# Second-key one-hots of the second token tile built on GpSimd instead of VectorE and ScalarE

## What is computed

```python
s_top, i_top = lax.top_k(sc, TOPK)                    # sc: scores of 8 heads x 2 x 128 keys
cand_idx = i_top[..., 0, :, None] * N_KEYS + i_top[..., 1, None, :]
best_s, best_pos = lax.top_k(cand.reshape(T, PEER_HEADS, TOPK * TOPK), TOPK)
g = jax.nn.softmax(best_s, axis=-1)                   # idx, g: 8 heads x 16 = 128 slots a token
u = peer_u[eb]                                        # gathered rows, (token, slot, 2048)
a = jax.nn.gelu(jnp.einsum('td,tkd->tk', xb, u), approximate=False)
return jnp.einsum('tk,tkd->td', wb * a, peer_v[eb])   # sum over the 128 slots of coef * row
h = layer_norm(ALPHA * h + ffn, ln2_g[l], ln2_b[l])
```

## Time and profile before

| | us |
|---|---|
| median of three runs | 2490.89 (2490.71 to 2491.93) |
| the profiled execution, its own time | 2489.8 |
| its span in the profile | 2487.9 |
| chunks of tile 1: first one-hot to the first panel matmul | 1940.41 to 1990.56 |
| panels and gathered rows: first panel matmul to the last row added | 1990.56 to 2468.6 |
| last layer norm and output | 2468.6 to 2487.9 |

### The profile page before, as it was taken

How to read it: one execution, slowest core, us unless ns; L and a number is a source line. 1 busy time by engine, 2 the same in 40 slices (tenths; PEclk the granted TensorE clock), 3 DMA queues, 4 the chain that set the end, 5 groups by cost and what they waited for, 6 DMA issues and landing times.

```text
span 2487.9 us, 28481 instructions
## 1 busy us (share of the span) xinstructions
PE 1769.2 (71%) x9808; PEld 1451.7 (58%) x9808; DVE 1678.8 (67%) x2299; ACT 792.8 (32%) x1339; POOL 1011.9 (41%) x559
## 2 busy tenths in 40 slices
PE   7999999999999999999700000012112699999996
PEld 5888999998889888888700000011112566666663
DVE  5444455554445555557899999999999866666666
ACT  4444444344444444455300010256347600000000
POOL 0000000000000000001388888888878078888884
PEclk9999999999999999999955555555555999999998
DMA  5444465556555555546999999999999299999997
GB/s 163 131 141 145 137 189 184 185 172 196 189 187 185 186 186 187 185 150 239 354 342 352 353 356 349 348 362 344 355 360 423 75 385 411 411 409 411 411 412 292
DMA packets 217046, 674.87 MB, mean 271 GB/s; under 512 B 18784, under 2 KB 68320, under 8 KB 183520
## 3 DMA queue, kind: packets, MB, share of 16 engines
q0 software_dynamic: 57488, 393.25, 41.4%
q1 hardware_dynamic: 159456, 280.32, 33.8%
HBM read 671.42 MB, written 2.10 MB: 271 GB/s over the span
## 4 chain that ended last, share of the span: by engine, by line
PE 45%; DVE 27%; issue 15%; POOL 8%; DMA 3%; ACT 1%; DVEq 0%; POOLq 0%; ACTq 0%; SPq 0%
PE ps L413 44%; DVE junk L1545 18%; POOL v_rows L1751 7%; DMA v_rows<-in_v_gathered,idx_all 2%; POOL u_rows L1738 1%; DVE ohs L1568 1%; DMA u_rows<-in_peer_u,idx_all 1%; ACT hi L835 1%; DVE lo L1209 0%; DVE oh_k L1524 0%; DVE ohv L1528 0%; DVE ohs L1565 0%; PE ps L498 0%; DVE ij_all L1532 0%; DVE h L1583 0%
## 5 line engine op out<-in xcount | busy, mean ns | idle before, releaser
L1209 DVE TENSOR_TENSOR lo<-raw,hi 128x1024 fp32r<-128x1024 f32 x368 | 448.7, 1225 | 490.1 <-ACT hi L835 488.7
L1738 POOL DMA_INDIRECT u_rows<-in_peer_u,idx_all x256 | 597.9, 2336 | 198.6 <-issue 107.6
L1545 DVE SCALAR_TENSOR_TENSOR junk<-u_rows,h 128x2048 bf16<-128x2048 f32 x256 | 584.7, 2291 | 47.2 <-DVE best L1514 3.5
L835 ACT ACTIVATE hi<-raw 128x1024 fp32r<-128x1024 f32 x376 | 397.6, 1060 | 567.9 <-PE ps L413 565.5
L413 PE MATMUL ps<-v_raw,wt 128*128 128x368 f32 x1536 | 475.4, 472 | 2.8 <-DMA v_raw<-in_peer_v 2.0
L1751 POOL DMA_INDIRECT v_rows<-in_v_gathered,idx_all x256 | 391.1, 1528 | 151.4 <-issue 78.2
L413 PE MATMUL ps<-xh,hi 128*128 128x256 f32 (+2 forms) x1536 | 440.6, 287 | 2.6 <-ACT qkv L835 1.3
L413 PE MATMUL ps<-xh,lo 128*128 128x256 f32 (+2 forms) x1536 | 435.6, 284 | 0.0
L413 PE MATMUL ps<-xl,hi 128*128 128x256 f32 (+2 forms) x1536 | 435.0, 283 | 0.0
L1583 DVE SCALAR_TENSOR_TENSOR h<-v_rows,coef_all,h 128x944 f32<-128x944 f32 x256 | 307.6, 1201 | 172.9 <-DMA v_rows<-in_v_gathered,idx_all 171.9
L413 PEld LDWEIGHTS ps<-v_raw,wt 128*128 128x128 f32 x1536 | 291.7, 190 | 186.1 <-DMA v_raw<-in_peer_v 2.8
(11 more groups left out here) (217 smaller groups left out, 2271.7 us busy)
## 6 DMA issues: line engine op xcount, KB each, us to landing
raw<-in_w_in SPq DMA_DIRECT2D x96, 1024.0 KB, 5.4
v_raw<-in_peer_v SPq DMA_DIRECT2D x128, 552.0 KB, 7.8
raw<-in_w_in SPq DMA_DIRECT2D x64, 256.0 KB, 3.2
raw<-in_w_in SPq DMA_DIRECT2D x32, 512.0 KB, 4.6
raw<-in_p_a SPq DMA_DIRECT2D x16, 1024.0 KB, 5.0
raw<-in_p_b SPq DMA_DIRECT2D x16, 1024.0 KB, 5.1
raw<-in_w_o SPq DMA_DIRECT2D x16, 1024.0 KB, 5.1
raw<-in_peer_wq SPq DMA_DIRECT2D x16, 1024.0 KB, 6.7
```

Source lines behind the costliest of these rows:

```text
L835: return nc.scalar.activation(o, i, f, **kw)
L1209: V.tensor_tensor(raw_lo[:, hh // 2, k4, :] if kept else lo[:, hh % SLOT_N, :, :], raw[:, hh // 2, k4, :], (kept_hi(hh) if kept else hi[:, ...
L1545: V.scalar_tensor_tensor(junk[:, n % 2, :], u_rows[k % (RING if u else HEAD_RING)][:, :], 1.0, h1[:, u // PH, :], ALU.mult, ALU.mult, accu ...
L1738: Q.indirect_dma_start(u_rows[slot][:, :], None, peer_u, bass.IndirectOffsetOnAxis(ap=idx_all[:, n:n + 1], axis=0)).then_inc(u_in[slot], 16)
```

## The change

The second-key one-hots of tile 1 go to POOL for all 32 chunks, as four `tensor_scalar` with `is_equal`, one for each token, with the key as a [128, 1] operand. DVE loses its 24 `tensor_tensor`, ACT its eight `key_one_hots` (four squares and a Relu each). PE waits for POOL's semaphore beside DVE's. POOL gathers the rows 0 to 2 as before, waits for `slots_copied`, makes the chunks 32 to 36, gathers the rows 3 and 4, makes the chunks 37 to 63, and then gathers the row 5 and the rest. `gather_v` itself is the same.

```diff
@@ place(c), on PE
                     pe.wait_ge(S("oh_dve_ready"), c - CHUNKS_T + 1)
-                    if c % 4 == ACT_B:
-                        pe.wait_ge(S("oh_ready"), CHUNKS_T + (c - CHUNKS_T) // 4 + 1)
+                    pe.wait_ge(S("oh_pool_ready"), c - CHUNKS_T + 1)
@@ end of the block of ScalarE
             slots_copy(1)
-            key_one_hots(CHUNKS_T + ACT_B)
             for c in range(CHUNKS_T, 2 * CHUNKS_T):
                 w_copy(c)
-                if c % 4 == 0 and c > CHUNKS_T:
-                    key_one_hots(c + ACT_B)
@@ one_hots(c), on VectorE
-                if c % 4 != ACT_B:
-                    V.tensor_tensor(o[:, 1, :, :], iota[:, :].unsqueeze(1).to_broadcast([P, WB, P]),
-                                    slots_t[:, 2, t0:t0 + WB].unsqueeze(2).to_broadcast([P, WB, P]), ALU.is_equal)
                 for q in range(WB):
@@ end of the block of GpSimd
-            for n in range(NT * SLOTS):
+            def key_one_hots(c):
+
+                pool.wait_ge(S("w_done"), c - OHR + 1)
+                t0 = c % CHUNKS_T * WB
+                for q in range(WB):
+                    ins = Q.tensor_scalar(oh[c % OHR][:, 1, q, :], iota[:, :], slots_t[:, 2, t0 + q:t0 + q + 1], None,
+                                          ALU.is_equal)
+                ins.then_inc(S("oh_pool_ready"), 1)
+
+            for n in range(3):
+                gather_v(n)
+            pool.wait_ge(S("slots_copied"), 2)
+            for c in range(CHUNKS_T, 2 * CHUNKS_T):
+                key_one_hots(c)
+                if c == CHUNKS_T + 4:
+                    gather_v(3)
+                    gather_v(4)
+            for n in range(5, NT * SLOTS):
                 gather_v(n)
```

More of the change, by code:

```diff
@@ L78 @@
 OHR = 3
-ACT_B = 3
 Y_CUTS = ((FD, D), (0, 2 * CW), (2 * CW, FD))
@@ L280, in decoder_layer @@
                   "scaled tile_opened acc_scaled slots_turned slots_copied "
-                  "one_hot_squares one_hot_units oh_ready oh_dve_ready w_done w_evac vr_in0 vr_in1 vr_in2 vr_in3 vr_in4 "
+                  "one_hot_squares one_hot_units oh_ready oh_dve_ready oh_pool_ready w_done w_evac vr_in0 vr_in1 vr_in2 vr_in3 vr_in4 "
                   "panel_done v_added ln2_stats ln2_rstd ln2_half y2_ready").split():
@@ L1142, in one_hots @@
                 ins.then_inc(S("oh_ready"), 1)
[L1144 to L1154, removed]
             def w_copy(c):
```

## The result

The changed kernel takes 2526.45 us (median of four runs, 2525.99 to 2527.28) where the kernel before takes 2491.41 beside it: a ratio of 1.0141, 95% interval 1.0123 to 1.0159. The forecast was 2499 and its range ended at 2519. The sign was right, the size was not: 35 us instead of 8.

What follows compares the result with a forecast made beforehand. POOL was to become the bound of tile 1's chunks: 48.6 us of one-hots, 2.6 for two gathers and 4.6 beside row adds, 55.8 in place of 47.9, giving 2499 us; range 2482 to 2519.

Steps and rivals of the forecast that it cites:

- A slope: In POOL's one-hot step: growth of 0.88 ns a column, taken from affine_selects of 1024 and 128 columns.
- an overlap: In POOL's one-hot step: 0.07 us of each duration hides behind its neighbour, taken from two memsets.
- the rows' bounds: For one POOL one-hot in tile 1's stream: a step between 0.245 and 0.67 us, of which 0.38 was taken.
- a rival's range: Tile 1's chunks: VectorE's and POOL's one-hots exclude each other, step 0.58 to 0.67 us, time 2524 to 2536; chance 0.10.

## What to carry to other kernels

Work moved to an idle engine has to be priced per column with that very operation on that engine: a copy and a `tensor_scalar` of one shape differed by 2.4 times on GpSimd (0.24 and 0.58 us for 128 columns). A slope needs two rows of one operation on the same partitions, and an overlap two instructions of the kind that will follow each other. Where the trace has no row for it, the range must reach as far as the rows' bounds do; a 50 us stretch made of 128 equal instructions multiplies every error in one. And where a measured time lands in a rival's range, run the case that takes the rival's cause away before believing it.

## What the runs showed of the hardware

- GpSimd's `tensor_scalar` in float32: 0.58, 0.414 and 0.337 us from start to start with 128, 64 and 32 columns; a constant instead of a per-partition operand (0.61) or a multiply instead of the compare (0.59) changes little. A copy of 128 columns takes 0.24.
- A GpSimd instruction whose listed time is shorter (0.53 with the constant) can have the same step: time it from start to start.
- A GpSimd one-hot beside VectorE's row adds of two SBUF inputs gets in once in 1.33 us, one for each add.
- GpSimd also holds VectorE up: 92 VectorE one-hots in 37.82 us, one in each GpSimd step, at 64 columns. At 128 columns it holds it up little (four in 1.23 us), and beside a copy they don't grow (341 ns).
